# A decoder layer whose residual is turned from rows of tokens to rows of channels

## The chip, the core and the metric

The kernel runs on one core of a Trainium2 chip. A core has a matmul engine (TensorE, PE in the profile; PEld is its loading of weights), a vector engine (VectorE, DVE), an activation engine (ScalarE, ACT), GpSimd (POOL) and a sync engine (SP). SP and POOL do hardly any arithmetic here: they issue DMA transfers, each in its own written order, and 16 DMA engines carry these. Matmuls multiply a stationary operand (the weights, at most 128x128) with a moving one (up to 512 columns) into one of eight PSUM banks of 128 x 512 fp32. All data are fp32, and one matmul in the program is two records in the trace.

The metric is the device time of one call in microseconds (us). Lower is better.

## What is computed

One layer of a decoder for a prompt of 256 tokens and 8 samples of one token each, so 264 tokens, of width 2048. Cut to what matters:

```python
def _rms(x, g):                       # three times: before mix, cross, experts
    return x * rsqrt(mean(x * x, -1) + EPS) * g
z = _rms(x, g_mix) @ w_in             # 2048 -> q 768 | k 768 | v 768 | u 1280
# q, k, v: 12 heads of 64, QK-norm, window attention with bias; a sample reads
#   its cache of 2048 keys at three dilations (128, 97 and 96 rows matter)
# u: 4 groups x 320; trailing mean over 2/4/8/16 tokens minus the token,
#   then a 320x320 map per group and a scale per channel
x = x + concat(attention, pooled) @ w_out          # 2048 -> 2048
q = rms_heads(_rms(x, g_cross) @ w_cq)             # 4 heads of 128
x = x + cross_attention(q, mem_k, mem_v) @ w_co    # 256 memory rows
x = x + experts(_rms(x, g_ffn))       # top 1 of 4 groups, top 2 of 8 experts
```

The caches of window keys and values are outputs too: 8 samples x 2 caches of 6141 KB, copied from DRAM to DRAM. Each of the 32 experts has 12.6 MB of weights, and all are read.

## The kernel before

There is no scheduler: each engine has its own hand-written list of instructions, and semaphores tie the lists together. The work runs in stages:

1. Constants, the memory rows and `x` are loaded. `norm_turn` (L634) normalises and turns rows at once: a matmul with a 128x128 block of rows stationary and a diagonal matrix of scales moving. DVE puts the result into `hT` in `norm_rows` (L1325), times the gain.
2. `project` (L640) multiplies with w_ck and w_cv (memory keys and values), then with w_in in seven chunks of 512 columns. The 128 tokens of a tile are stationary, 512 weight columns stream past, 16 k-steps for each of two token tiles; the eight samples come by themselves in `project_sample` (L647). Six matmuls (L705) turn the bias between chunks. During chunks 4 to 6 `query_row` (L679) spreads a sample's query over 128 partitions, and DVE multiplies and sums it with the keys (`sample_scores`, L1352 and L1355).
3. `attend` runs the 12 heads one after another: `score_win`, `turn_win`, `value_win`.
4. Pooling is done on PE: `pool_channels` (L789 to L792) multiplies `u` with constant matrices; `pool_map` (L810) applies the maps. `values_of` (L819) sums each sample's values.
5. w_out in four chunks, again by `project` and `project_sample`; DVE adds the rows to the residual `x3`.
6. `norm_turn`, w_cq, cross attention of four heads; w_co, with the samples' cross attention between (L679, L819).
7. `norm_turn`, the router (L941), and then 32 experts in a loop: gather (L969), gate and up (L1028), down (L1053), combine (L993).

The residual `x3` lies by tokens: 128 tokens on the partitions, 2048 channels along each.

SP brings the large weights through a ring of two slots of 4 MB (`big`, L391): the piece i + 2 is issued when piece i has been used by PE. Once w_cq and w_co have been used, their two slots take the first expert's gate and up halves (L470), and the stream of expert weights begins: each half is fetched again when the expert before has used it. POOL issues the sixteen cache copies (`cache_copy`, L531), each after a named weight piece has landed, and between them, in one list, the rows of window keys and values (`window_rows`, L541 to L544) and of the memory caches (L594). A POOL instruction that waits holds everything behind it in this list.

Of the kernel before, what the change touches and what calls it, by code (L numbers as in the profile page):

```python
# [8 lines left out]
F32 = mybir.dt.float32  # L9
# [6 lines left out]
P = 128  # L16
# [6 lines left out]
TC = SEQ + 32  # L23
# [32 lines left out]
def bias_columns(dist):  # L56
# [3 lines left out]
    for c, d in enumerate(dist):  # L60
# [4 lines left out]
        else:  # L65
# [10 lines left out]
CONST_W = dict(ident=P, tri=P, moe=NE + NE + 3 + OVB + BLK, pool=PG * 256 + PG * P, pools=2 * PG * NB,  # L76
               flip=P, mask=AW, xmask=XW, sel=4, ohp=384, ohs=NDEC)
# [8 lines left out]
def constants():  # L86
# [17 lines left out]
    full = np.zeros((PG, SEQ, SEQ), np.float32)  # L104
    for g, w in enumerate(POOL_WINDOWS):
        for t in range(SEQ):
            lo = max(t + 1 - w, 0)
            full[g, lo:t + 1, t] = 1.0 / min(w, t + 1)
            full[g, t, t] -= 1.0
    pool = part("pool")  # L110
    pool[:, 0:PG * 256] = full[:, 0:P].transpose(1, 0, 2).reshape(P, -1)
    pool[:, PG * 256:] = full[:, P:, P:].transpose(1, 0, 2).reshape(P, -1)
    ps = part("pools").reshape(P, 2, PG, NB)
    for g, w in enumerate(POOL_WINDOWS):
        for b in range(NB):
            ps[b * HIST + HIST - (w - 1):b * HIST + HIST, 0, g, b] = 1.0 / w
            ps[b, 1, g, b] = 1.0 / w - 1.0
    for i in range(4):
        for h in range(H):
            part("mask")[32 * i + h, h * HD:(h + 1) * HD] = 1.0  # L120
        for h in range(XH):
            part("xmask")[32 * i + h, h * XD:(h + 1) * XD] = 1.0
        part("sel")[32 * i:32 * i + 32, i] = 1.0
    part("ohp")[0:NBUCKET + 1] = bias_columns([255 - v for v in range(384)])
    part("ohs")[0:NBUCKET + 1] = bias_columns(DEC_DIST)
    return c


def hybrid_decoder_layer(nc, a):
    with ExitStack() as ctx:  # L130
# [3 lines left out]
        def sb(name, shape, dt=F32):  # L134
            return ctx.enter_context(nc.sbuf_tensor(name, shape, dt))

        bias_dram = nc.dram_tensor("bias_rows", (H, 384), F32, kind="Internal").ap()


        ring = sb("ring", [P, 3, 8192])
        x3 = sb("x3", [P, 3, D])
        hT = sb("hT", [P, KT, TC])
        z = sb("z", [P, 3, IN_W])
        qkm = sb("qkm", [P, 4096])
        mkT = qkm[:, H * SEQ:].rearrange("p (h m) -> p h m", h=XH)
        qkT = qkm[:, 0:H * SEQ].rearrange("p (a h t) -> p a h t", a=2, h=H // 2)
        ident = sb("ident", [P, P])
        tri = sb("tri", [P, P])  # L150
        dg = sb("dg", [P, 3, P])
# [3 lines left out]
        poolsc = sb("poolsc", [P, 2, PG, NB])  # L155
        sel = sb("sel", [P, 4])
        gT = sb("gT", [P, 4, KT])
        gqk = sb("gqk", [P, 2, HD])
        gxx = sb("gxx", [P, 2, XD])
        psc = sb("psc", [P, PW // P])  # L160
        st = sb("st", [P, 152])
# [3 lines left out]


        slot2 = ring[:, 2, :]
        mixT = slot2[:, 0:KT * TC].rearrange("p (k t) -> p k t", k=KT)
        hmT = slot2[:, 0:KT * NM].rearrange("p (k t) -> p k t", k=KT)
        AFTER_MIX = KT * TC  # L170
        bias = slot2[:, AFTER_MIX:AFTER_MIX + H * SEQ].rearrange("p (h j) -> p h j", h=H)
        bias_flat = after_mix = slot2[:, AFTER_MIX:AFTER_MIX + H * SEQ]
        biasS = slot2[:, AFTER_MIX + H * SEQ:AFTER_MIX + H * SEQ + NDEC]
        qkt_flat = qkm[:, 0:H * SEQ]
        rb = psm[:, 0, 0:H]
        rbs = psm[:, 0, 16:144].rearrange("p (i h) -> p i h", i=4)
        flip = slot2[:, 8192 - P:8192]
        hankel = qkt_flat
        ohp = qkt_flat[:, 0:384]
        ohs = qkt_flat[:, 384:384 + NDEC]  # L180
        brow = qkt_flat[:, 768:768 + 384]
        sq = qkt_flat[:, 1536:1536 + 2 * AW]
        zf = z[:].rearrange("p t n -> p (t n)")
# [6 lines left out]
        pw = pslot[:, 0:10 * PC].rearrange("p (c d) -> p c d", c=10)  # L190
        poolT = pslot[:, 3200:3200 + 10 * TOK].rearrange("p (c t) -> p c t", c=10)
        state = pslot[:, 5840:5840 + PW]
        poolc = z[:, 0, 0:2 * AW]
        poolA = poolc[:, 0:1024].rearrange("p (g t) -> p g t", g=PG)
        poolB = poolc[:, 1024:1536].rearrange("p (g t) -> p g t", g=PG)
        prb = z[:, 1, 0:768].rearrange("p (b j) -> p b j", b=2)
        prT = z[:, 1, 768:1536].rearrange("p (b j) -> p b j", b=2)
        h_flat = hT[:].rearrange("p k t -> p (k t)")

        kbuf, vbuf = ([r[:, lo:lo + 3 * AW].rearrange("p (t n) -> p t n", t=3) for r, lo in rs]  # L200
                      for rs in (((slot2, 0), (slot2, 3 * AW)), ((h_flat, 0), (h_flat, 3 * AW), (qkt_flat, 0))))
        norm_dump = h_flat[:, 0:D]
        mask = after_mix[:, 0:AW]
        masked = after_mix[:, AW:2 * AW]

        memr = zf[:, 0:2 * D].rearrange("p (t n) -> p t n", t=2)
        msq = zf[:, 2 * D:2 * D + XW]
        mk = z[:, 2, IN_W - 4 * XW:IN_W - 2 * XW].rearrange("p (t n) -> p t n", t=2)
        mv = z[:, 2, IN_W - 2 * XW:IN_W].rearrange("p (t n) -> p t n", t=2)
        xq = zf[:, 0:3 * XW].rearrange("p (t n) -> p t n", t=3)  # L210
        xqT = zf[:, 1536:1536 + XH * SEQ].rearrange("p (h t) -> p h t", h=XH)
        xsq = zf[:, 2560:2560 + XW]
        oT = slot2[:, 0:XH * TC].rearrange("p (h t) -> p h t", h=XH)
        xprb = slot2[:, 1152:2176].rearrange("p (b j) -> p b j", b=2)
        xprT = slot2[:, 2176:3200].rearrange("p (b j) -> p b j", b=2)

# [74 lines left out]
        def wk(i):  # L291

            return ring[:, i % 2, :].rearrange("p (k n) -> p k n", k=KT)
# [1452 lines left out]
```

## Time and profile before

| | us |
|---|---|
| median of 3 runs | 1753.99 |
| range of the runs | 1750.31 to 1757.3 |
| the profiled execution, its own time | 1755.72 |
| its span in the trace | 1753.9 |
| PE busy in it | 1395.7 |
| PE loading weights | 659.6 |
| DVE busy | 582.6 |
| ACT busy | 177.0 |
| POOL busy | 55.2 |

The span leaves out 1.8 us that lie around it. Busy times of PE and PEld overlap. A busy share over the whole span mixes stages with different limits, so the stages are to be read one by one. In a view by windows, the granted clock is a share of TensorE's full speed, and the DMA share is the mean busy share of the 16 DMA engines.

### The profile page before, as it was taken

How to read it: one execution, taken by the hardware profiler on the slowest of the kernel's cores; microseconds unless marked ns; L12 is line 12 of the kernel's file. 1: busy time of each engine (PE TensorE's matmuls, PEld its weight loads, DVE VectorE, ACT ScalarE, POOL GpSimd, SP SyncE). 2: the span in 40 equal slices, each digit the busy share in tenths (PEclk: the TensorE clock that was granted, in tenths of full speed). 3: DMA queues.
4: the chain of work that ended last, by engine and by line, in shares of the span. 5: the costliest groups of instructions: out<-in, count | busy, mean ns of one | idle time of the engine just before them, and what ended most of it. 6: DMA issues, size and time to landing. Idle time of an engine off the chain costs nothing.

```text
span 1753.9 us, 24539 instructions
## 1 busy us (share of the span) xinstructions
PE 1395.7 (80%) x10597; PEld 659.6 (38%) x10597; DVE 582.6 (33%) x1157; ACT 177.0 (10%) x439; POOL 55.2 (3%) x103
## 2 busy tenths in 40 slices
PE   5999999889999987885867777777677776767675
PEld 4474454445454564462322222222232222222222
DVE  2120244352000023644433434343434343434344
ACT  2000010033100003110000000000000000000000
POOL 0000011111110000100000000000000000000000
PEclk9999999977999998986988989898989898999898
DMA  7997479989289999553999999999999999999996
GB/s 304 332 327 247 155 247 358 274 303 293 78 281 330 336 335 342 185 215 137 413 427 424 428 424 428 425 428 424 428 424 428 424 428 425 427 425 427 426 427 265
DMA packets 80539, 607.56 MB, mean 346 GB/s; under 512 B 12128, under 2 KB 15662, under 8 KB 44493
## 3 DMA queue, kind: packets, MB, share of 16 engines
q1 hardware_dynamic: 72349, 480.87, 67.2%
q0 software_dynamic: 8144, 126.02, 21.2%
q8 instruction: 36, 0.59, 0.1%
q14 instruction: 10, 0.08, 0.0%
HBM read 601.84 MB, written 106.16 MB: 404 GB/s over the span
## 4 chain that ended last, share of the span: by engine, by line
PE 48%; DMA 45%; DVE 4%; SPq 1%; issue 1%; ACT 1%; DVEq 0%; POOL 0%; ACTq 0%
DMA ring<-in_w_e_up_dram 41%; PE pb L640 22%; PE pb L1028 9%; PE pb L634 4%; DMA ring<-in_w_in_dram 3%; PE pb L647 2%; PE pb L819 2%; PE pb L810 1%; SPq L470 1%; PE pb L679 1%; PE pb L775 1%; PE pb L766 1%; PE pb L969 0%; PE pb L941 0%; PE pb L789 0%
## 5 line engine op out<-in xcount | busy, mean ns | idle before, releaser
L1028 PE MATMUL pb<-ring,z 128*32 128x256 f32 x4096 | 310.8, 471 | 194.5 <-DMA ring<-in_w_e_up_dram 193.8
L1679 DVE TENSOR_TENSOR x<-pb,x 128x512 f32<-128x512 f32 (+1 forms) x384 | 237.5, 678 | 398.6 <-PE pb L993 398.6
L1028 PEld LDWEIGHTS pb<-ring,z 128*32 128x32 f32 x4096 | 153.6, 134 | 375.2 <-DMA ring<-in_w_e_up_dram 245.8
L640 PE MATMUL pb<-ring,hT 128*128 128x512 f32 x512 | 227.0, 603 | 10.7 <-DMA ring<-in_w_in_dram 9.6
L640 PE MATMUL pb<-ring 128*128 128x512 f32 x448 | 196.7, 598 | 1.6 <-DVE ring L1325 0.8
L640 PEld LDWEIGHTS pb<-ring,hT 128*128 128x128 f32 x512 | 98.3, 194 | 132.3 <-issue 121.2
L640 PEld LDWEIGHTS pb<-ring 128*128 128x128 f32 x448 | 85.3, 192 | 108.1 <-issue 106.2
L1053 PE MATMUL pb<-ring,z 128*32 128x512 f32 x992 | 114.6, 603 | 0.0
L993 PE MATMUL pb<-z 32*128 32x512 f32 (+1 forms) x768 | 106.0, 622 | 3.9 <-issue 2.2
L969 PE MATMUL pb<-z 128*32 128x512 f32 (+1 forms) x792 | 100.1, 620 | 6.3 <-DVE z L1658 6.3
L634 PE MATMUL pb<-dg,x 128*128 128x128 f32 x288 | 64.3, 392 | 17.2 <-DVE dg L1316 17.2
L634 PEld LDWEIGHTS pb<-dg,x 128*128 128x128 f32 x288 | 63.4, 312 | 20.1 <-DVE dg L1316 18.0
L1262 ACT ACTIVATE z<-pb 128x128 f32<-128x128 f32 x32 | 8.9, 277 | 521.3 <-PE pb L1028 521.3
L1691 DVE TENSOR_SCALAR z<-z 128x128 f32<-128x128 f32 x32 | 7.3, 227 | 160.4 <-ACT z L1262 160.4
L1486 DVE TENSOR_TENSOR x<-pb,x 128x512 f32<-128x512 f32 x16 | 11.1, 692 | 123.1 <-PE pb L640 123.1
L1053 PEld LDWEIGHTS pb<-ring,z 128*32 128x32 f32 x992 | 29.5, 111 | 57.6 <-issue 57.0
L1417 DVE COPY z<-pb 128x512 f32<-128x512 f32 x7 | 4.8, 691 | 124.7 <-PE pb L640 124.7
L1034 PE MATMUL pb<-ident,z 128*128 128x128 f32 x32 | 10.7, 334 | 40.4 <-DVE z L1697 40.4
L969 PEld LDWEIGHTS pb<-z 128*32 128x32 f32 (+1 forms) x792 | 19.3, 109 | 60.4 <-issue 50.3
L977 PE MATMUL pb<-ident,z 128*128 128x128 f32 x132 | 21.2, 285 | 26.1 <-ACT z L1258 26.1
L993 PEld LDWEIGHTS pb<-z 32*128 32x128 f32 (+1 forms) x768 | 23.8, 149 | 36.7 <-issue 34.1
L1352 DVE TENSOR_TENSOR ring<-ring,pb 128x1536 f32<-128x1536 f32 (+1 forms) x16 | 20.9, 1350 | 48.4 <-PE pb L679 48.4
(251 smaller groups left out, 1017.2 us busy)
## 6 DMA issues: line engine op xcount, KB each, us to landing
ring<-in_w_e_gate_dram SPq DMA_DIRECT2D x64, 2048.0 KB, 19.0
ring<-in_w_e_up_dram SPq DMA_DIRECT2D x64, 2048.0 KB, 23.5
ring<-in_w_e_down_dram SPq DMA_DIRECT2D x31, 4096.0 KB, 22.1
out_win_k_sample_dram<-in_cache_win_k_dram POOLq DMA_DIRECT2D x8, 6141.0 KB, 22.3
out_win_v_sample_dram<-in_cache_win_v_dram POOLq DMA_DIRECT2D x8, 6141.0 KB, 24.7
ring<-in_w_in_dram SPq DMA_DIRECT2D x7, 4096.0 KB, 16.7
ring<-in_w_out_dram SPq DMA_DIRECT2D x4, 4096.0 KB, 17.5
ring<-in_cache_win_k_dram POOLq DMA_DIRECT2D x16, 288.0 KB, 8.3
```

Of the source, the lines that this page charges most:

```text
L470: sp.dma_start(ring[:, half, 4096 * m:4096 * m + 4096].rearrange("p (k n) -> p k n", k=8), src.rearrange("(p k) n -> p k n", k=KT)[:, 8 * ...
L634: last = mm(bk[:, P * k:P * k + P], cols[:, 4 * j + k, :], dg[:, t, :], start=True, stop=True)
L640: last = mm(bk[:, :], xT[:, k, tile * P:tile * P + P], w[:, k, :], start=(k == 0), stop=(k == nk - 1))
L647: last = mm(bk[32 * c:32 * c + 32, 0:P], xT[:, k, SEQ:TC], w[:, k, P * c:P * c + P], start=(k == 0), stop=(k == nk - 1))
L819: last = mm(bk[32 * i:32 * i + 32, 0:n], s_in[0:k, t, hf, 32 * i:32 * i + 32], buf[0:k, t, lo:lo + n], start=(t == 0), stop=(t == len(tile ...
L969: last = mm(pb[0][32 * c:32 * c + 32, :], pick[0:n, t, :], xn[0:n, t, 512 * c:512 * c + 512], start=(t == 0), stop=(t == 2))
L977: last = nc.tensor.transpose(pb[0][:, P * j:P * j + P], xe[:, P * j:P * j + P], ident[:])
L993: last = mm(banks[c][0:n, :], GT[r, P * t:P * t + n], yo[r, :], start=True, stop=True)
L1028: last = mm(pb[1][32 * c:32 * c + 32, 0:256], XT[:, k % 4, 32 * (k // 4):32 * (k // 4) + 32], w[:, :, k8, P * c:P * c + P], start=(k == 0) ...
L1053: last = mm(pb[3][32 * c:32 * c + 32, :], aT[:, 32 * f:32 * f + 32], w[f][:, 512 * c:512 * c + 512], start=(f == 0), stop=(f == 3))
L1352: V.tensor_tensor(src, src, filled()[:, 0:n].unsqueeze(1).to_broadcast([P, tiles, n]), ALU.mult)\
L1679: last = V.tensor_tensor(d, banks[c][0:n, :], d, ALU.add)
```

## The change

The residual is kept by channels instead, as `xT`: 128 channels on the partitions, 16 blocks of channels, 264 tokens along each.

- Rows are turned once, by plain transposes of `x` and of the memory rows; the norms' scales are spread by a matmul with ones, and DVE writes `hT` in 16 instructions of 264 columns (`scaled_rows`). Sums of squares come from ACT squares, added up on DVE.
- The projections onto `u`, w_out, w_cq and w_co keep a 128x128 block of weights stationary and stream the 264 tokens past it, prompt and samples together: `channels` (10 tiles of 16 steps), the w_out loop (16 tiles of 16), `cross_query` (4 of 16), the w_co loop (16 of 4). The projections onto q, k, v (four and a half chunks of w_in) and of the memory stay as they were.
- Window attention goes by pairs of heads, and its steps stand between the tiles of `channels`.
- Pooling's trailing sums are shifted adds on DVE (`pool_sums`, `pool_mean`), and only the samples' old state goes over PE.
- The samples' queries are stored in DRAM and read back by a DMA that spreads them over 128 partitions (`qrep`); `query_row` is gone, and so are the matrices of constants and masks that were loaded for pooling and for `own_heads`.
- The samples' window values go in three column groups of one bank. Their cross attention is grouped: the keys are transposed between the w_out tiles, and one bank takes all samples' scores.
- The router's matmuls take the residual by channels and run beside the w_co tiles; for the experts the rows are turned back to tokens.
- POOL's list is written anew. The expert loop and the order of its weights are as they were; two of the cache copies now wait until the first expert's first half has landed.

PE's list in window attention. Before, one head after another (L759 and L760 scores, L766 turns of the probabilities, L775 and L776 values):

```order
L759 MATMUL pb<-qkm 128x128
L760 MATMUL pb<-qkm 128x256
L766 MATMUL pb<-ident,z 128x128 x3
L775 MATMUL pb<-z 64x256
L776 MATMUL pb<-z 64x128
```

In the changed kernel, at the same place, with L737 the channel tile, L784 the values, L775 the turns and L766 the scores of a pair:

```order
L784 MATMUL pb<-Z 64x256 x2
L784 MATMUL pb<-Z 64x128 x2
L775 MATMUL pb<-ident,Z 128x128 x6
L766 MATMUL pb<-qkm 128x128 x2
L766 MATMUL pb<-qkm 128x256 x2
L737 MATMUL pb<-hreg,ring 128x264 x16
```

The five steps of one head, which followed those of the head before, have become the steps of three different pairs with a whole weight tile behind them.

POOL's list at the fifth and sixth cache copies, with the semaphore that an entry waits for (w_landed is a landed weight piece, keys_used a sample's keys used by DVE). Before:

```order
L531 DMA out_win_k_sample_dram<-in_cache_win_k_dram 96x16376 [waits w_landed1]
L541 DMA ring<-in_cache_win_k_dram 128x768 [waits keys_used]
L542 DMA ring<-in_cache_win_k_dram 96x768
L543 DMA ring<-in_cache_win_k_dram 96x768
L544 DMA ring<-z 1x16x48
L541 DMA ring<-in_cache_win_k_dram 128x768 [waits keys_used]
```

And in the changed kernel, where L550 is the copy and L564 the spread query:

```order
L550 DMA out_win_v_sample_dram<-in_cache_win_v_dram 96x16376 [waits w_landed0]
L554 DMA ring<-in_cache_win_k_dram 128x768 [waits keys_used]
L555 DMA ring<-in_cache_win_k_dram 96x768
L556 DMA ring<-in_cache_win_k_dram 96x768
L557 DMA ring<-out_win_k_sample_dram 1x16x48
L564 DMA Z<-sample_queries 128x768
L554 DMA ring<-in_cache_win_k_dram 128x768 [waits keys_used]
```

The rows of keys still stand behind a copy in one list, with one more transfer for each sample, and the next copy stands behind two samples' rows instead of three.

PE's list at the end of w_out. Before, L640 the prompt, L647 the samples, L634 the norm:

```order
L640 MATMUL pb<-ring 128x512 x32
L647 MATMUL pb<-ring 32x128 x64
L634 MATMUL pb<-dg,x 128x128 x48
L640 MATMUL pb<-ring,hT 128x512 x16
```

In the changed kernel, with L890 the w_out tile, L897 the turn of memory keys, L901 the norm's sum and L909 the cross query:

```order
L890 MATMUL pb<-hreg,ring 128x264 x10
L890 MATMUL pb<-Z,ring 128x264 x6
L897 MATMUL pb<-ident,qkm 128x128 x4
L901 MATMUL pb<-Z,ones 128x264
L909 MATMUL pb<-hreg,ring 128x264 x32
```

The 48 norm matmuls between w_out and w_cq have become one, and the turns of the memory keys have come into the w_out loop.

The diff, cut to its core:

```diff
-            def norm_turn(rows, first, end, parts=range(4), new_scales=True):
-                for t in range(first, end):
-                    cols = rows[:, t, :].rearrange("p (m k) -> p k m", k=KT)
-                    for j in parts:
-                        bk = vbank()
-                        for k in range(4):
-                            last = mm(bk[:, P * k:P * k + P], cols[:, 4 * j + k, :], dg[:, t, :], start=True, stop=True)
+            for k in range(KT):
+                bk = abank("x")
+                for t in range(2):
+                    turn(bk[:, P * t:P * t + P], xraw[:, t, P * k:P * k + P], ident[:])
+                turn(bk[:, SEQ:TOK], xraw[0:NB, 2, P * k:P * k + P], ident[0:NB, 0:NB]).then_inc(a_filled, 1)
...
-            def norm_rows(first, end, gain, dst, parts=range(4)):
-                        V.tensor_tensor(dst[:, 4 * j:4 * j + 4, P * t:P * t + n], src,
-                                        gT[:, gain, 4 * j:4 * j + 4].unsqueeze(2).to_broadcast([P, 4, n]), ALU.mult)\
+            def scaled_rows(i):
+                for k in range(KT):
+                    V.scalar_tensor_tensor(out=hT[:, k, :], in0=xT[:, k, :], scalar=gT[:, KT * i + k:KT * i + k + 1], in1=rbc[:],
+                                           op0=ALU.mult, op1=ALU.mult).then_inc(h_ready, 1)
...
-            for n in range(NCH):
-                project_sample(hT, wk(i), KT, abank(), a_filled)
+            for n in range(5):
+                width = 512 if n < 4 else 256
+                project_sample(wk(IN0 + n), abank("sin"), width // 4)
...
+            def channels(j):
+                c = 2 + j
+                if c % 4 == 0:
+                    piece_landed(pe, IN0 + 4 + c // 4)
+                w = wk(IN0 + 4 + c // 4)[:, :, P * (c % 4):P * (c % 4) + P]
+                bk = abank("u")
+                for k in range(KT):
+                    last = mm(bk[:, 0:TOK], w[:, k, :], hT[:, k, :], start=(k == 0), stop=(k == KT - 1))
+                last.then_inc(a_filled, 1)
...
-            attend(H, score_win, turn_win, value_win)
+            channels(3)
+            channel_rows(0, 3)
+            value(0)
+            turn_probs(1)
+            score(2)
...
-            def query_row(rows, lo, n, b):
-                mm(bk[:, 0:n], ident[:, b:b + 1].to_broadcast([P, P]), rows[:, 2, lo:lo + n], start=True, stop=True)\
+                pool.dma_start(qrep[:, b % 2], qs_dram[b:b + 1, :].to_broadcast([P, AW])).then_inc(key_landed[b % 2], 16)
...
+                link(TT(rows, rows, qrep[:, b % 2].unsqueeze(1).to_broadcast([P, 3, AW]), ALU.mult))
...
-            def pool_channels(c):
-                    mm(bk[o, 0:SEQ], z[:, 0, u], poolA[:, g, :], start=True, stop=False)
-                    mm(bk[o, P:SEQ], z[:, 1, u], poolB[:, g, :], start=False, stop=True)
-                    mm(bk[o, SEQ:TOK], state[0:NB * HIST, us], poolsc[0:NB * HIST, 0, g, :], start=True, stop=False)
-                    last = mm(bk[o, SEQ:TOK], z[0:NB, 2, u], poolsc[0:NB, 1, g, :], start=False, stop=True)
+            def pool_sums(tiles, levels, only_last=None):
+                link(TT(S0[:, 0:n, 1:UC], uT[:, j0:j0 + n, 1:UC], uT[:, j0:j0 + n, 0:UC - 1], ALU.add))
+                for lv in range(1, levels):
+                    src, dst = (S0, S1) if lv % 2 else (S1, S0)
+                    link(TT(dst[:, i, lo:UC], src[:, i, lo:UC], src[:, i, lo - d:UC - d], ALU.add))
...
-                        last = mm(bk[32 * i:32 * i + 32, 0:n], s_in[0:k, t, hf, 32 * i:32 * i + 32],
-                                  buf[0:k, t, lo:lo + n], start=(t == 0), stop=(t == len(tiles) - 1))
+                    for g in range(VG):
+                        last = mm(sv[32 * g:32 * g + 32, 0:VC], pvals(t, n, b, g), vbuf[b % 3][0:n, t, VC * g:VC * g + VC],
+                                  start=(b == 0 and t == 0), stop=(b == NB - 1 and t == 2))
...
-                project(mixT, wk(i), KT, 0, vbank(), v_filled)
-                project(mixT, wk(i), KT, 1, vbank(), v_filled)
-                project_sample(mixT, wk(i), KT, vbank(), v_filled)
+            for o in range(KT):
+                w = wk(WOUT + o // 4)[:, :, P * (o % 4):P * (o % 4) + P]
+                    last = mm(bk[:, 0:TOK], w[:, k, :], mix(k), start=(i == 0), stop=(i == KT - 1))
+                if t == 0:
+                    pe.wait_ge(xk_landed[b % 2], 16 * (b // 2 + 1))
+                    last = turn(bk[:, P * h:P * h + P], xk[b % 2][:, t, XD * h:XD * h + XD], ident[:])
...
-                    query_row(xq, 0, XW, 2 * n + t)
+                    last = mm(bk[32 * h:32 * h + NB, 0:NM], qown[:, h, b, :], KT8[:, b, h, :], start=(b == 0), stop=(b == NB - 1))
...
-                    project(oT, wo[:, :, 512 * n:512 * n + 512], XH, t, vbank(), v_filled)
+                    last = mm(pb[o % 4][:, 0:TOK], wo[:, h, P * o:P * o + P], oT[:, h, :], start=(h == 0), stop=(h == XH - 1))
+                last = mm(pb[4][0:36, 0:TOK], wr[:, k, :], xT[:, k, :], start=(k == 0), stop=(k == KT - 1))
...
-                    for i in range(10, 16):
-                        piece_landed(pool, WOUT + (2, 3, 4, 4, 5, 5)[i - 10])
-                        cache_copy(i)
+            for i in range(14, 16):
+                pool.wait_ge(gu_landed[0], 32)
+                cache_copy(i)
```

## Rows read from the trace of the kernel before

**Rows 1.** The page's own line of busy times, and the chain's shares by line.
```profile
PE 1395.7 (80%) x10597; PEld 659.6 (38%) x10597; DVE 582.6 (33%) x1157; ACT 177.0 (10%) x439; POOL 55.2 (3%) x103
...
DMA ring<-in_w_e_up_dram 41%; PE pb L640 22%; PE pb L1028 9%; PE pb L634 4%; DMA ring<-in_w_in_dram 3%; PE pb L647 2%; PE pb L819 2%; PE pb L810 1%; SPq L470 1%; PE pb L679 1%; PE pb L775 1%; PE pb L766 1%; PE pb L969 0%; PE pb L941 0%; PE pb L789 0%
```

**Rows 2.** Timeline of SP's queue: start, us, engine, line, transfer.
```profile
823.98 0.34 SPq L470 DMA_DIRECT2D ring<-in_w_e_gate_dram  x1
```

**Rows 3.** Windows: stretch, length, busy PE, PEld, DVE, ACT, POOL; clock, DMA share, GB/s.
```profile
0.00:824.00 824.00, 736.05 (x3757) 407.63 (x3761) 224.89 (x458) 110.12 (x279) 55.18 (x103) 0.93 0.77 266
...
113.40:363.30 249.90, 240.33 (x1398) 119.47 (x1399) 69.22 (x58) 16.30 (x41) 19.75 (x38) 0.98 0.77 256
363.30:419.00 55.70, 48.19 (x175) 29.48 (x172) 27.68 (x107) 28.46 (x90) 7.36 (x15) 0.60 1.00 339
419.00:487.40 68.40, 67.62 (x276) 34.10 (x275) 2.04 (x4) 8.56 (x21) 11.04 (x21) 1.00 0.42 126
487.40:614.30 126.90, 126.89 (x768) 62.64 (x768) 8.95 (x20) 6.50 (x18) 6.76 (x11) 0.99 0.93 327
614.30:697.50 83.20, 67.05 (x345) 46.97 (x345) 26.32 (x67) 18.43 (x46) 1.01 (x2) 0.90 0.97 342
697.50:783.40 85.90, 69.91 (x360) 44.34 (x360) 45.84 (x76) 13.96 (x38) 7.85 (x11) 0.90 0.51 190
783.40:824.00 40.60, 22.07 (x141) 9.70 (x145) 19.12 (x79) 1.00 (x3) 0.00 (x0) 0.66 0.32 127
824.00:1754.00 930.00, 659.64 (x6848) 252.01 (x6840) 357.75 (x699) 66.93 (x160) 0.00 (x0) 0.90 0.99 417
```

**Rows 4.** Chain of waits, first 125 us: start, us, what.
```profile
20.67 14.25 PE pb L634 x64
...
35.69 55.20 PE pb L640 x128
90.89 20.86 PE pb L634 x96
111.74 0.87 PE pb L672 x8
```

**Rows 5.** The same chain over the whole span.
```profile
113.39 13.97 PE pb L640 x32
...
277.87 47.84 DMA ring<-in_w_in_dram
```

**Rows 6.** Timeline of PE, three short stretches.
```profile
447.84 0.94 PE L810 MATMUL pb<-ring 128*128 128x264 f32 x3 [0.47 <-ACT ring L1183]
...
447.84 1.16 PE L810 MATMUL pb<-ring 128*128 128x264 f32 x4 [0.47 <-ACT ring L1183]
...
783.43 7.31 PE L941 MATMUL pb<-hT,z 128*36 128x264 f32 x32 [0.38 <-DVE hT L1325]
...
419.32 4.07 PE L819 MATMUL pb<-hT,s_in 128*32 128x512 f32 x12
```

**Rows 7.** Groups of VectorE by form: busy us, mean ns.
```profile
L1352 DVE TENSOR_TENSOR ring<-ring,pb 128x768 f32<-128x768 f32 x8 | 7.6, 947 | 0.0
...
L1465 DVE SCALAR_TENSOR_TENSOR z<-pb,ring 128x256 f32<-128x256 f32 x12 | 5.0, 413 | 0.0
```

**Rows 8.** DMA issues with us to landing: page, line L391, and window 373 to 440.
```profile
out_win_k_sample_dram<-in_cache_win_k_dram POOLq DMA_DIRECT2D x8, 6141.0 KB, 22.3
...
DMA to landing us min/median/max: 13.5/19.0/62.4
...
ring<-in_w_out_dram SPq DMA_DIRECT2D x1, 4096.0 KB, 62.4
```

**Rows 9.** Chain of waits, 600 to 860 us.
```profile
620.29 21.24 PE pb L634 x96
...
697.48 3.70 PE pb L640 x8
701.18 0.86 PE pb L679 x2
```

More of the change, by code:

```diff
@@ L198, in hybrid_decoder_layer @@
[L198 to L208, printed above, removed]
@@ L465, in gate_up @@
+            for i in range(WOUT + 1, CO + 1):
+                big(i)
             def gate_up(i, e, half):
@@ new lines, in score @@
+            def score(p):
+                if p == 0:
+                    pe.wait_ge(a_freed, a_at("qk", 5))
+                banks = [vbank("score"), vbank("score")]
+                for lo, rows, n in ((0, slice(0, P), P), (P, slice(P, SEQ), SEQ)):
+                    for i in range(2):
+                        r = slice(64 * i, 64 * i + 64)
+                        last = mm(banks[i][:, lo:lo + n], qkT[r, 0, p, rows], qkT[r, 1, p, 0:n], start=True, stop=True)
+                        if lo:
+                            last.then_inc(v_filled, 1)
@@ L795, in pool_map @@
+            piece_landed(pe, POOLW)
+            pe.wait_ge(state_landed, 16)
+            bk = vbank("state")
+            for g in range(PG):
+                for j, r, n in GROUP[g]:
+                    last = mm(bk[r:r + n, NB * j:NB * j + NB], state[0:NB * HIST, P * j + r:P * j + r + n],
+                              poolsc[0:NB * HIST, g, :], start=True, stop=True)
+            last.then_inc(v_filled, 1)
             def pool_map(kt):
-                bk = abank()
+                pe.wait_ge(pooled, 1 if kt < 7 else 2)
+                bk = abank("map")
+                parts = []
@@ new lines, in _ @@
+            last.then_inc(a_filled, 1)
+            cross_turn(2)
+            cross_value(1)
+            pe.wait_ge(a_freed, a_at("xsturn"))
+            pe.wait_ge(xv_landed, 16 * NB)
+            bk = abank("xsvals")
+            for b in range(NB):
+                for t in range(2):
+                    for h in range(XH):
+                        last = mm(bk[32 * h:32 * h + NB, 0:XD], pown[:, t, h, b, :], xv[b][:, t, XD * h:XD * h + XD],
+                                  start=(b == 0 and t == 0), stop=(b == NB - 1 and t == 1))
@@ new lines, in _, with channels, channel_rows @@
+                for c in range(4):
+                    last = copy(z[0:NB, 2, 512 * n + w * c:512 * n + w * c + w], bk[32 * c:32 * c + NB, 0:w])
+                freed(last)
+            def channels(j):
+                freed(copy(uT[:, j, PAD:UW], filled("u")[:, 0:TOK]))
+            def channel_rows(first, end):
+                bk = filled("uout")
+                for j in range(first, end):
+                    r, lo = (32, 2 * AW + P * j) if j < 6 else (64, 2 * AW + P * (j - 6))
+                    last = copy(z[r:r + 32, 2, lo:lo + P], bk[0:32, P * (j - first):P * (j - first) + P])
+                freed(last)
@@ new lines, in _ @@
+            cross_exps(2)
+            cross_turned(1)
+            cross_exps(3)
+            act.wait_ge(s_biased, 3)
+            nc.scalar.activation(xps, VB[(v_at("xsscore") - 1) % 4][:, 0:NM], ACT.Exp, bias=st[:, 112:113], scale=-1.0,
+                                 accum_out=st[:, 114:115]).then_inc(s_exped, 1)
+            cross_value(0)
+            bk = filled("xsturn")[:, 0:2 * P].rearrange("p (t h c) -> p t h c", t=2, h=XH)
+            act.wait_ge(own_zero, 1)
+            for t in range(2):
+                last = copy(p_flat[:, t, :, 0:NB * NB:NB + 1], bk[:, t, :, 0:NB])
```

1695 lines of the change are left out of this document (925 added, 770 removed).

## The prediction

> **What bounds the kernel now.** I read the page first [rows 1]: PE is busy for 80% of the span, but the chain's largest entry is a DMA, the experts' up weights, with 41%. A mean over two different programs, then, and the question is where they meet. SP's queue gives the place: at 823.98 us it issues the first weights of the expert stream [rows 2]. The windows show what each half is limited by [rows 3]. From 824 to the end, 930 us, the DMA engines are busy for 0.99 of the time at 417 GB/s: that half lasts as long as its weights take. Before it, PE is busy for 736 of 824 us, and the DMA engines for only 0.77. So
>
> time = start of the expert stream + 930,
>
> and all that the change can win lies before the start. The change leaves the experts, their weights and their order alone, so 930 stays. What can pull the start forward is PE's path, and what can stop it is the DMA work ahead of the start: 0.77 x 824 = 634 us of fully busy engines [rows 3]. Hence two sums: PE's path without any wait for DMA, and then the waits.
>
> **PE's path, part by part.** The price of the new form, 264 columns with a new 128x128 weight for every record: three such records take 0.94 us and four 1.16 [rows 6], so one more costs 0.22; the router's 32 records (36 weight columns) take 7.31, 0.228 each [rows 6]. I take 0.222; a tile of 16 steps (32 records) is 7.1 us.
>
> 1. Entry. The 20.86 us of norm matmuls for `x` between the memory projections and w_in go [rows 4]. In their place 48 transposes stand ahead of the memory projections, at 0.109 each (8 in 0.87 [rows 4]) 5.2 us, with 32 for the memory rows, 3.5 us; together less than the 14.25 that 64 records take there now [rows 4], though the loads and the statistics come first as before. I let the memory projections start at 37 instead of 35.7, add 55.2 and 3 us for a slower clock and eight key transposes: w_in starts at 95 instead of 113.4. The 16 scaled writes on DVE (413 ns for 256 columns [rows 7], so 6.8 us) lie beside the memory projections.
> 2. q, k, v: the first chunk's tile takes 13.97 [rows 5]; with the other tile and the samples a chunk is 31.2. Four chunks 125, half a chunk 17, the bias matmuls 5: 147, to 242.
> 3. Channels and attention. Ten tiles are 71 us. Before, attention's stretch of 55.7 us had PE busy for 48.2 at a granted clock of 0.60 [rows 3], so at full clock at most 29; two heads of a pair now use different halves of the array, for which I take 22. With 3 for turns, 96: to 338. The pooling matrices go; 12 shifted adds and some ten small corrections on DVE cost about 16 us (947 ns for 768 columns [rows 7]) on an engine busy for 27.7 of 55.7 there, and hide behind the tiles, save the last group, which the maps wait for; 2 us for that.
> 4. Samples' values, state and maps took 68.4 [rows 3]. The constants' matmuls leave; a sample's values, 12 records of up to 512 columns in 4.07 [rows 6], become 18 of 256 in three column groups, about 1.5 to 2; ten maps about 1.8. Sum 34: to 372.
> 5. w_out: 16 tiles 114, and 64 key transposes 7: 121 instead of 126.9 [rows 3], to 493. The gain is small: 264 columns in place of two times 512 and the samples' pass, but a new weight each time. DVE adds each tile to the residual and ACT squares it, some 0.4 to 0.5 us of 264 columns each [rows 7], beside 7.1 of PE.
> 6. Norm, w_cq and cross attention: 83.2 before [rows 3]. The 21.24 of norm matmuls [rows 9] go; one sum, a root and 16 paced writes (12 us, the first query tile rides along), three more tiles (21), heads and grouped samples (33): 66, to 559.
> 7. w_co: 128 records 28.4, router 7.3, turning back 5.2: 41, to 600, instead of 85.9 [rows 3]. The query rows (0.86 after each 3.70 of w_co [rows 9]) and the samples' pass are gone.
> 8. Router to first half used: 40.6 before [rows 3], less the 7.3 that moved up and 2 of norm, is 31; plus 6 for building the rows and scales again: 637.
>
> PE's path alone would start the stream at 637, 187 us earlier, and end at 1567.
>
> **What of that the DMA engines give back.** Their work ahead of the start grows by the spread queries (8 x 0.39 MB) and shrinks by constants and masks: I take 634 + 5 = 639, with 634 and 650 as bounds. A path of 637 with 639 of transfers under it would need engines that never rest, and the order forbids that: the ring has two slots, a weight piece is issued only when one is free, and copies are issued when a weight piece lands. A cache copy takes 22.3 us to land [rows 8], and while one runs a weight piece hardly advances: a piece needs 13.5 alone, but 47.84 behind a copy and key rows [rows 5], 62.4 behind others at the worst [rows 8]. Today that costs PE one long wait; the pieces will now be used every 28 to 31 us as before, but the stages between, which gave the engines time (419 to 487 at a DMA share of 0.42, 697 to 783 at 0.51 [rows 3]), shrink by half. Walking the queues by these prices:
> - the third channel tile waits for w_in's sixth piece, behind the sixth copy and key rows: 12 us;
> - the turns of pairs 1 and 4 stand behind DVE's sample scores in DVE's list, and these behind key rows that POOL issues after a copy: 17 and 15 us. What is held there is PE's list, and all later tiles;
> - in w_out the memory keys stand in POOL's list behind copies, and PE's key transposes wait for them between the tiles: 14 us;
> - 13 us for a lower granted clock after such waits (0.60 to 0.90 in the stretches that have them now, 0.99 to 1.00 in those that don't [rows 3]).
>
> Sum 71: the start moves to 708. As a check, the DMA engines then rest for 708 - 639 = 69 us ahead of the start, against 190 now (a share of 0.90 instead of 0.77). Bounds: no waits, 637; all the rest kept, share 0.77, 639 / 0.77 = 830.
>
> 708 + 930 = 1638 of span; the 1.8 us around it and the profiled run's distance from the median (1755.72 against 1753.99) cancel. Forecast **1638 us**, 6.6% faster; its own range is 1600 to 1680, for waits of 33 to 113 us.
>
> **A rule against the change.** Both forms take a fresh weight in every record. A record of 512 columns takes 13.97/32 = 0.437 us [rows 5], one of 264 takes 0.222 [rows 6]; 0.437 x 264/512 is 0.225, so the time goes with the columns and nothing is left over for the load. The Trainium skill, page "TensorE: Matmul & The Clock Gate", Part 3 "The mechanism", says that a weight load overlaps a running matmul only when the two use different row groups; these use the same 128 rows. By its section "LDWEIGHTS (loading the stationary operand)" a load of 128 columns takes 107 ns, an estimate from which would make a record 0.33. The trace does not bear this out; I keep it as a rival, since a run of four is short and the router's weights have only 36 columns.
>
> **Rivals.**
> - *PE's path alone decides* (1565 to 1600). For it: in 487 to 614 PE is busy for 126.89 of 126.90 us with the DMA at 0.93 [rows 3]. Against: it would want the DMA engines at 0.95 and more over the whole first part, which no long stretch there has.
> - *More waits* (1680 to 1745): a share of about 0.86, start 743, 1673, and upward to 0.78, 1749. For it: the waits couple, since a late PE frees a slot late, the piece after it lands late, and so does the copy that waits for it. Against: copies have been spread so that their rows come sooner in POOL's list.
> - *Nothing won* (1745 to 1763): the DMA share stays at 0.77, start 830.
> - *Loads not hidden*: 1088 records (320 channels, 512 w_out, 128 w_cq, 128 w_co) at 0.105 more are 114 us on PE's path, of which half falls into the waits: start about 768, 1698. The router's 32 records at 0.228 speak against it [rows 6].
> - *Slower, by the clock*: in 363 to 419 a PE with small matmuls between waits had a granted clock of 0.60 [rows 3]. If the many short waits kept it there through channels, w_out, cross and w_co, some 340 us of matmuls at full clock would take 340/0.60 = 567: path 637 + 227 = 864, end 1794. It decides from 297 + 340/c = 824, a clock of 0.65. For it: attention's steps now stand between the tiles. Against: the same stages as dense tiles hold 0.98 to 1.00 [rows 3], and the tiles are now in among the small steps.
>
> **How the numbers follow.** Forecast 0.60; PE's path alone 0.13; more waits 0.14; loads not hidden 0.04; nothing won 0.03; slower by the clock 0.06. A difference of 0.5%, 8.8 us, is about what a measurement of this kernel can tell from none. Faster by more: 0.60 + 0.13 + 0.14 + 0.04 = 0.91; within it 0.03; slower 0.06. The range 1580 to 1715 leaves out under half of PE's path alone (0.05), under half of more waits (0.06) and the last two (0.09): 2 in 10.
>
> **What would show it.** In the changed trace the first SP issue of the second expert's gate weights should stand near 708, with 930 after it. The channel and w_out tiles should take 7.1 us each (10.6 if loads are not hidden). The window from the start of w_in should begin near 95. PE's idle time should be put down to window key rows, the sixth piece of w_in and memory keys, some 55 to 60 us in all, and the DMA share ahead of the start should be near 0.90. I am wrong if the tiles are slow, if the start lies above 790 or below 650, or if the part after it is not 930.

## The result and the profile after

The changed kernel takes 1649.79 us (median of 4 runs, 1648.75 to 1652.41), against 1752.6 us for the kernel before, timed beside it: a ratio of 0.9412, 95% interval 0.9389 to 0.9436, or 5.9% faster. The forecast was 1638, with a range of 1580 to 1715. The profiled run has a span of 1648.1 us.

First the place where the two programs meet. SP's timeline of the changed kernel (start, us, engine, line, transfer), the row that answers to [rows 2]:

```profile
715.46 0.33 SPq L489 DMA_DIRECT2D ring<-in_w_e_gate_dram  x1
```

The stream starts 108.5 us earlier than before, and 932.6 us follow it, where 930 did. The time is won ahead of the stream, all of it. The windows of the changed kernel, cut where its stages begin (columns as in [rows 3]):

```profile
0.00:98.10 98.10, 78.38 (x228) 40.33 (x229) 23.18 (x57) 22.02 (x37) 1.36 (x6) 0.91 0.90 304
98.10:243.20 145.10, 145.10 (x969) 77.09 (x968) 37.04 (x34) 13.37 (x33) 12.63 (x24) 1.00 0.94 329
243.20:380.90 137.70, 101.79 (x507) 81.22 (x505) 60.04 (x122) 30.44 (x101) 18.49 (x35) 0.85 0.96 311
380.90:423.30 42.40, 38.83 (x245) 19.56 (x243) 5.88 (x16) 5.31 (x13) 13.94 (x25) 0.88 0.87 268
423.30:564.50 141.20, 126.65 (x576) 106.92 (x576) 12.61 (x32) 14.20 (x32) 10.07 (x15) 0.94 0.84 298
564.50:630.70 66.20, 54.73 (x381) 41.66 (x381) 24.36 (x46) 15.65 (x43) 2.19 (x5) 0.87 0.94 354
630.70:674.60 43.90, 43.85 (x196) 29.17 (x196) 12.12 (x31) 11.04 (x25) 0.00 (x0) 1.00 1.00 363
674.60:715.50 40.90, 15.08 (x128) 7.72 (x131) 17.36 (x80) 16.57 (x13) 0.00 (x0) 0.62 0.42 180
715.50:1648.00 932.50, 658.92 (x6848) 252.36 (x6840) 357.82 (x699) 67.16 (x160) 0.00 (x0) 0.90 0.99 416
```

Read the PE column against the length. In q, k and v (98 to 243), and in w_co (631 to 675), PE is busy throughout. In channels and attention (243 to 381) it is busy for 101.8 of 137.7 us at a clock of 0.85, with the DMA engines at 0.96: there PE waits for DMA. In the last 41 us ahead of the stream PE is busy for 15.1, and the DMA engines have a share of 0.42.

What PE waits for, the four longest between w_in and the stream (engine, line, tile, what it waits for: us in all, times, longest):

```profile
PE pb L775 <- DVEq L1569: 25.4, 2, 16.4
PE pb L1034 <- DVE xT L1794: 15.2, 1, 15.2
PE pb L897 <- DMA qkm<-in_cache_mem_k_dram: 14.0, 3, 7.9
PE pb L737 <- DMA ring<-in_w_in_dram: 9.8, 1, 9.8
```

The first row names DVE, but the chain of waits shows what DVE had waited for (start, us, what; the sixth piece of w_in, the two waits for spread queries, one wait for memory keys in w_out with the weight piece ahead of it, and a w_out tile):

```profile
228.41 43.31 DMA ring<-in_w_in_dram
...
274.58 27.00 DMA Z<-sample_queries
...
320.11 23.17 DMA Z<-sample_queries
...
477.84 7.14 PE pb L890 x32
484.99 28.99 DMA ring<-in_w_out_dram
514.81 23.55 DMA qkm<-in_cache_mem_k_dram
```

The spread query of a sample is the last transfer of its key rows. It took 27.0 and 23.2 us behind cache copies that POOL had issued 2.6 and 5.4 us earlier; in the run without copies below it lands after 4.4 to 11.7 us. In w_out the order is the same: POOL waits for the weight piece, issues a copy at 514.27, and the memory keys come behind it. The row of L890 is a w_out tile: 32 records in 7.14 us, 0.223 each.

A wait costs PE more than its own length. The tile behind the wait for w_in's piece ran at a mean granted clock of 0.74, the next one at 1.00; from PE's timeline, in which a tile at the full clock takes 7.3 to 7.4:

```profile
271.77 9.88 PE L737 MATMUL pb<-hreg,ring 128*128 128x264 f32 x32 [9.75 <-DMA ring<-in_w_in_dram]
...
283.09 7.39 PE L737 MATMUL pb<-hreg,ring 128*128 128x264 f32 x32
```

### The profile page after: what moved, and what is told of

It is laid out like the page before. It is cut to its first block, busy times and chain, and to the rows that moved or that the text cites. A ratio compares the mean times of both kernels' runs of the same rounds, so it can differ in the third digit from the quotient of the medians.

```text
span 1648.1 us, 23510 instructions
## 1 busy us (share of the span) xinstructions
PE 1263.3 (77%) x10061; PEld 656.0 (40%) x10061; DVE 550.4 (33%) x1117; ACT 195.8 (12%) x454; POOL 58.7 (4%) x109
## 4 chain that ended last, share of the span: by engine, by line
DMA 54%; PE 37%; DVE 4%; SPq 2%; ACT 2%; issue 1%; POOL 0%; DVEq 0%; POOLq 0%; ACTq 0%
DMA ring<-in_w_e_up_dram 43%; PE pb L1111 11%; PE pb L663 10%; PE pb L890 4%; DMA Z<-sample_queries 3%; DMA qkm<-in_cache_mem_k_dram 3%; DMA ring<-in_w_in_dram 3%; PE pb L909 2%; PE pb L1009 2%; DMA ring<-in_w_out_dram 2%; SPq L429 1%; PE pb L858 1%; PE pb L737 1%; PE pb L669 1%; SPq L489 1%
## 5 line engine op out<-in xcount | busy, mean ns | idle before, releaser
L1111 PE MATMUL pb<-ring,xT 128*32 128x256 f32 x4096 | 312.8, 473 | 197.7 <-DMA ring<-in_w_e_up_dram 196.9
L1868 DVE TENSOR_TENSOR Z<-pb,Z 128x512 f32<-128x512 f32 (+1 forms) x384 | 237.6, 679 | 389.9 <-PE pb L1076 389.9
L1111 PEld LDWEIGHTS pb<-ring,xT 128*32 128x32 f32 x4096 | 154.9, 135 | 378.9 <-DMA ring<-in_w_e_up_dram 248.1
L663 PE MATMUL pb<-ring,hreg 128*128 128x512 f32 (+1 forms) x320 | 125.3, 551 | 0.0
L1136 PE MATMUL pb<-ring,xT 128*32 128x512 f32 x992 | 112.8, 595 | 0.0
L1076 PE MATMUL pb<-xT 32*128 32x512 f32 (+1 forms) x768 | 106.0, 622 | 3.8 <-issue 2.1
L1052 PE MATMUL pb<-Z,xT 128*32 128x512 f32 (+1 forms) x792 | 97.9, 608 | 6.3 <-DVE xT L1847 6.3
L737 PE MATMUL pb<-hreg,ring 128*128 128x264 f32 x320 | 78.9, 408 | 9.8 <-DMA ring<-in_w_in_dram 9.8
L890 PE MATMUL pb<-hreg,ring 128*128 128x264 f32 x320 | 77.9, 401 | 0.3 <-ACT Z L1302 0.3
L737 PEld LDWEIGHTS pb<-hreg,ring 128*128 128x128 f32 x320 | 63.9, 202 | 23.9 <-DMA ring<-in_w_in_dram 10.2
L890 PEld LDWEIGHTS pb<-hreg,ring 128*128 128x128 f32 x320 | 62.5, 200 | 10.9 <-issue 0.4
L663 PE MATMUL pb<-ring 128*128 128x512 f32 x128 | 57.8, 615 | 0.0
L1136 PEld LDWEIGHTS pb<-ring,xT 128*32 128x32 f32 x992 | 29.1, 109 | 56.3 <-issue 55.6
L890 PE MATMUL pb<-Z,ring 128*128 128x264 f32 x192 | 45.3, 386 | 0.0
L890 PEld LDWEIGHTS pb<-Z,ring 128*128 128x128 f32 x192 | 36.5, 190 | 6.2
```

The lines of the kernel that those rows point to most:

```text
L663: last = mm(bk[:, 0:n], xt[:, k, tile * P:tile * P + P], w[:, k, 0:n], start=(k == 0), stop=(k == KT - 1))
L737: last = mm(bk[:, 0:TOK], w[:, k, :], hT[:, k, :], start=(k == 0), stop=(k == KT - 1))
L890: last = mm(bk[:, 0:TOK], w[:, k, :], mix(k), start=(i == 0), stop=(i == KT - 1))
L1052: last = mm(pb[0][32 * c:32 * c + 32, :], pick[0:n, t, :], xn[0:n, t, 512 * c:512 * c + 512], start=(t == 0), stop=(t == 2))
L1076: last = mm(banks[c][0:n, :], GT[r, P * t:P * t + n], yo[r, :], start=True, stop=True)
L1111: last = mm(pb[1][32 * c:32 * c + 32, 0:256], XT[:, k % 4, 32 * (k // 4):32 * (k // 4) + 32], w[:, :, k8, P * c:P * c + P], start=(k == 0) ...
```

## Experiments

Each run is timed beside the kernel before. Where several runs were taken, the median and the ratio to the kernel before are given; the two can differ by some us when they are set against the changed kernel, and then both are named.

**1. The changed kernel without copies.**

```diff
-                pool.dma_start(dst.rearrange("(p f) -> p f", p=96), src.rearrange("(p f) -> p f", p=96)).then_inc(copied, 16)
+                return
```

> The changed kernel without its sixteen cache copies (98 MB that it then does not move; the two sample cache outputs stay unwritten). Theory: the start of the expert stream is PE's path plus what DMA takes from it. In the changed kernel PE idles 25.4 us for sample scores held by key rows, 9.8 for the sixth piece of w_in, 14.0 for memory keys and about 3 for value rows, and runs some 10 us slower after these. Without copies all of that goes: start from 715 to about 652, time about 1586 (1575 to 1605). Rival: the waits come from the order of the lists on PE, DVE and ACT, not from the copies: start stays above 700, time above 1630.

1587.2 us (one run); the stream starts at 651.63, as expected. The theory holds and the rival falls. The windows, cut at the same stages:

```profile
0.00:96.70 96.70, 76.26 (x228) 38.76 (x229) 22.81 (x57) 21.89 (x37) 0.20 (x4) 0.93 0.59 200
96.70:242.90 146.20, 146.20 (x975) 78.07 (x974) 37.24 (x35) 13.47 (x33) 10.72 (x20) 1.00 0.53 183
242.90:336.70 93.80, 92.48 (x500) 74.52 (x499) 60.12 (x122) 30.23 (x101) 17.01 (x32) 1.00 0.61 189
336.70:378.90 42.20, 37.42 (x246) 19.12 (x245) 5.87 (x16) 5.30 (x13) 13.89 (x25) 0.92 0.83 269
378.90:501.10 122.20, 121.18 (x576) 103.53 (x576) 13.03 (x33) 14.37 (x33) 8.48 (x12) 1.00 0.53 191
501.10:566.90 65.80, 54.83 (x382) 41.84 (x382) 23.92 (x45) 15.11 (x41) 0.00 (x0) 0.87 0.49 198
566.90:610.80 43.90, 43.90 (x197) 29.15 (x197) 12.12 (x31) 11.04 (x25) 0.00 (x0) 1.00 0.14 52
610.80:651.60 40.80, 14.97 (x123) 7.63 (x127) 17.34 (x80) 16.57 (x13) 0.00 (x0) 0.62 0.36 150
```

Behind the entry PE waits for DMA for only 4.5 us here, all of it at the values, so this is the direct measure of the first of the two sums of the prediction. The run takes away both the copies' share of the engines and their place in POOL's list; it doesn't part the two. The copies cost the changed kernel 63.9 us of its path: 43.9 in channels and attention, 19.0 in w_out, 1 in the rest.

**2. The kernel before without copies.** The same edit to the kernel before.

> The kernel before, without its sixteen cache copies (same part left out). Theory: its PE path is the limit there, DMA only takes the wait for w_in's sixth piece and w_out's start (about 10 us of idle PE, and a low clock after it): 1725 to 1742, so far less than the same cut gives in the changed kernel. Rival: the kernel before was held by DMA as much as the changed one is: about 1690.

1743.39 us (one run), 10 us less than with copies and 1.4 outside the expected stretch; the stream starts at 809.01, 15 us earlier. The rival (1690) falls. The same 98 MB that hold the changed kernel back by 63 us cost the kernel before 10: it was PE's, and the changed one is PE's and DMA's together.

**3. Every channel tile twice.**

```diff
-                for k in range(KT):
+                for k in [*range(KT), *range(KT)]:
```

> The changed kernel with every channel tile computed twice into the same bank (the second pass starts afresh, so the values are the same): 71 us more of matmul between the steps of attention. Theory: 35 us of PE's waits there (pairs 1 and 4, sixth piece) are for DMA and are filled by the extra work, and the clock stays up: 25 to 45 us slower, about 1685. Rival: PE's list is the limit there and the waits move along: 65 to 71 slower, about 1718.

1680.15 us (one run), 30 us more for 71 us of added matmul, inside the expected 25 to 45. The rest went into waits that vanished: PE is busy for 163.5 of 164.7 us of this stage at full clock.

```profile
243.80:408.50 164.70, 163.53 (x819) 135.41 (x818) 60.12 (x122) 30.33 (x101) 18.42 (x35) 1.00 0.81 260
```

So the changed kernel's channel stage had some 41 us of free PE time, lost to waits and to the lower clock that came with them; the run without copies gives 43.9 for the same stage.

**4. The experts' rows behind the router.**

```diff
             rows_back(3)
+            act.wait_ge(exp_in, 1)
+            nc.scalar.activation(rt[:, 1300:1312], rt[:, 1300:1312], ACT.Exp).then_inc(exp_out, 1)
+            act.wait_ge(exp_in, 2)
+            nc.scalar.activation(rt[:, 1312:1315], rt[:, 1312:1315], ACT.Exp).then_inc(exp_out, 1)
+
             act.wait_ge(scale_ready, 1)
             act.wait_ge(back_copied, 12)
...
                               st[0:n, 9 + t:10 + t]).then_inc(xn_ready, 1)
-
-            act.wait_ge(exp_in, 1)
-            nc.scalar.activation(rt[:, 1300:1312], rt[:, 1300:1312], ACT.Exp).then_inc(exp_out, 1)
-            act.wait_ge(exp_in, 2)
-            nc.scalar.activation(rt[:, 1312:1315], rt[:, 1312:1315], ACT.Exp).then_inc(exp_out, 1)
```

> The changed kernel with ACT's three writes of the experts' rows (11.0 us) put behind the router's two exponentials instead of ahead of them. In the changed kernel DVE waits 7.7 us for the first exponential. Theory: the stream's start comes forward by that: 6 to 8 us faster, about 1642.5. Rival: the second half of the first expert's weights, which lands at 689, or the rows, then 3 us later than needed, hold it: 0 to 2 us.

1640.71 us (1633.55 to 1643.8), ratio 0.934 (0.9317 to 0.9363): 9 us faster than the changed kernel by the medians, 13 by the ratios, for an expected 6 to 8; in the profiled runs the stream starts 6.1 us earlier, at 709.38. The rival (0 to 2) falls. What had stood there, from the changed kernel's timeline (start, us, engine, line, out, in, count):

```profile
678.08 11.00 ACT L1393 ACTIVATE Z<-Z,st 128x2048 f32<-128x2048 f32 x3
...
689.10 1.28 ACT L1397 ACT_TABLE_LOAD   x1
690.39 0.21 ACT L1397 ACTIVATE xT<-xT 128x12 f32<-128x12 f32 x1
690.71 0.17 DVE L1784 TENSOR_REDUCE xT<-xT 128x3 f32<-128x12 f32 x1 [7.72 <-ACT xT L1397]
```

DVE waited 7.72 us for an exponential of 0.21 us that stood in ACT's list behind 11 us of rows and 1.28 of loading a table of functions. With the order turned round, PE's wait for the router (15.2 us) is 7.5.

**5. Attention behind the channel tiles.** PE's list is shown; those of ACT and DVE are reordered to match it.

```diff
-            channels(1)
-            score(0)
-            channels(2)
-            turn_probs(0)
+            for j in range(1, 4):
+                channels(j)
+            channel_rows(0, 3)
...
+            score(0)
+            score(1)
+            turn_probs(0)
+            for p in range(2, PAIRS):
+                score(p)
+                value(p - 2)
+                turn_probs(p - 1)
```

> The changed kernel with window attention behind all ten channel tiles instead of between them, as it was before the change (DVE scores samples 3 to 7 beside the tiles, then does the heads). Theory: the tiles between the steps covered the heads' DVE and ACT work, but they also put DVE's sample scores, and so the key rows behind copies, into PE's way. Undone, the tiles run through but for the sixth piece (71 + 13), the last sample's keys still come only near 343, and 35 to 45 us of heads follow: 5 to 15 us slower than the changed kernel, 1655 to 1665. Rival: the interleaving is worth what attention by itself costs, 25 us or more (1675 and up). Second rival: it costs more than it covers, and undoing it is faster.

1667.25 us (1660.06 to 1667.7), ratio 0.9488 (0.9458 to 0.9518): slower than the changed kernel by 17 us in the medians, 2 over the expected stretch, and by 13 in the ratios, inside it; either way below the first rival's. So interleaving pays, by less than attention costs by itself. In the profiled run the stream starts 17.3 us later, at 732.72. The stage takes 147.0 us in place of 137.7, with PE busy for 103.4 of them, and the values behind it 50.7 in place of 42.4, at a clock of 0.76 instead of 0.88:

```profile
242.30:389.30 147.00, 103.37 (x499) 81.88 (x498) 53.55 (x112) 29.31 (x97) 18.41 (x35) 0.85 0.85 278
389.30:440.00 50.70, 43.36 (x248) 22.00 (x247) 12.78 (x27) 5.59 (x17) 13.93 (x25) 0.76 0.86 265
```

PE waits 21.2 us for w_in's pieces and 18.8 behind DVE here, 9.8 and 25.4 in the changed kernel. That the sample scores in PE's way are what keeps interleaving from paying more is not shown by this run.

**6. Copies cut in two between the rows.**

```diff
+            key_rows(4)
             piece_landed(pool, IN0 + 5)
-            cache_copy(6)
...
+            cache_copy(6, (0,))
+            key_rows(5)
+            cache_copy(6, (1,))
...
+                    h = b - 1
+                    cache_copy(9 + h // 2, (h % 2,))
```

> The changed kernel with the rows after the router (as in the fourth run), and with copies 6 to 11 cut into two halves each that stand between single samples' rows in POOL's list: the same bytes, but no row stands behind more than half a copy (about 10 us). Theory: PE's waits for key rows (25.4 us) and for memory keys (14.0) fall to less than half: 15 to 30 us faster than the fourth run, 1612 to 1626. Rival: the engines carry the same bytes and a weight piece or a row comes late elsewhere instead, the DMA share ahead of the start stays at 0.89: within 5 us of the fourth run, 1636 to 1646.

1647.05 us (1642.19 to 1647.82), ratio 0.9377 (0.9354 to 0.9401): no faster than the fourth run, rather slower (6 us), and 1 us above the rival's stretch. The theory failed, in the way its rival said. PE's waits in this run (columns as above):

```profile
PE pb L897 <- DMA ring<-in_w_out_dram: 21.3, 1, 21.3
PE pb L782 <- DVEq L1576: 17.3, 2, 12.9
PE pb L744 <- DMA ring<-in_w_in_dram: 13.1, 1, 13.1
PE pb L875 <- DMA ring<-Z: 9.6, 2, 8.1
```

The waits for memory keys are gone and those for key rows are smaller, but a w_out piece now comes 21.3 us late, w_in's piece 13.1 and the value rows 9.6. The DMA share ahead of the start is 0.88. The order of these transfers decided who waits; the sum did not fall: 61.3 us for these four rows, against 52.5 for key rows, memory keys, w_in's piece and value rows in the fourth run.

**7. The kernel before with plain turns.**

```diff
-                        last = mm(bk[:, P * k:P * k + P], cols[:, 4 * j + k, :], dg[:, t, :], start=True, stop=True)
+                        last = nc.tensor.transpose(bk[:, P * k:P * k + P], cols[:, 4 * j + k, :], ident[:])
```

> The kernel before with each norm matmul against the diagonal of scales replaced by a plain transpose (leaves out the norms' scale factors). One record in place of two: memory rows, x, cross and router turn in about half the time or as fast as DVE empties a bank (0.69 us): some 8.5 + 12.5 + 13 + 9 us of PE's path go. Theory: PE's path was the limit there, the DMA share of 0.77 leaves room, and it comes through whole: 1708 to 1716. Rival: the DMA engines give half of it back, as in the changed kernel: 1728 to 1735.

1714.42 us (one run), inside the stretch of the theory. The stream starts at 778.32, 45.7 us earlier, for some 43 expected to leave PE's path, and the time is 39.5 us shorter, mostly since the part behind the start took 934 us in this run instead of 930. The DMA share ahead of the start rises from 0.77 to 0.81: the kernel before had room for it.

**8. Copies one place later.** On top of the fourth run:

```diff
-            for b in range(4, 7):
+            for b in range(4, NB):
                 key_rows(b)
-            piece_landed(pool, IN0 + 6)
-            cache_copy(7)
-            key_rows(7)
...
-            cache_copy(8)
+            cache_copy(7)
...
+            piece_landed(pool, CQ)
+            cache_copy(11)
             pool.wait_ge(v_filled, v_at("out", KT - 1))
             memory_rows(1, 7, xv[7], xv_landed)
...
+            pool.wait_ge(gu_landed[1], 32)
+            cache_copy(15)
```

> The kernel of the fourth run with the copies from the seventh on moved one place back in POOL's list: none stands between the samples' key rows 4 to 7 but one, the twelfth is issued when w_cq has landed (ahead of the last memory rows, not behind them), and the last waits for the second half of the first expert. Same bytes. The fourth run's DMA engines rest for 16 us in its last 34 us before the stream and for 23 us in w_out; without copies the start was 652. Theory: rest that is filled there is taken off PE's waits: the wait of pair 4 (about 15 us) goes, and little comes back: start from 709 to 695 to 700, time 1626 to 1634. Rival (as the half copies showed): another wait takes its place, 1636 to 1646.

1628.1 us (1623.79 to 1630.88), ratio 0.9286 (0.927 to 0.9302). As expected; it beats both kernels. The stream starts at 694.12. The first part of this run, its last 33 us ahead of the stream, and the same stage in the fourth run:

```profile
0.00:695.00 695.00, 603.51 (x3237) 401.82 (x3241) 192.57 (x418) 128.33 (x294) 58.57 (x109) 0.92 0.91 317
661.20:694.10 32.90, 14.77 (x126) 7.35 (x128) 17.36 (x80) 16.48 (x13) 0.51 (x1) 0.69 0.96 375
...
675.00:709.00 34.00, 15.88 (x119) 7.50 (x123) 17.36 (x80) 16.48 (x13) 0.00 (x0) 0.60 0.51 216
```

The share of that stage goes from 0.51 to 0.96. PE's waits for key rows fall from 25.7 to 16.8 us, and the four waits counted for the fourth run from 52.5 to 39.6 together. The difference to the sixth run: there the same bytes stayed in the same stages, here they moved into time in which little else was carried.

**9. The seventh copy behind all key rows too.**

```diff
-            piece_landed(pool, IN0 + 5)
-            cache_copy(6)
             for b in range(4, NB):
                 key_rows(b)
+            piece_landed(pool, IN0 + 6)
+            cache_copy(6)
```

> As the eighth run, and the seventh copy too stands behind the last key rows and the last piece of w_in instead of behind the sixth piece. Theory: both waits for key rows (25 us) and part of the wait for the last w_in piece go, the value rows come later by half a copy: 8 to 14 us faster than the eighth run, 1614 to 1624. Rival: with a copy less ahead of it the engines rest in attention, and what is put off is paid in w_out or at the values: within 4 us of the eighth run.

On top of the eighth run. 1630.0 us (1620.04 to 1640.62), ratio 0.93 (0.9269 to 0.933): no different from the eighth run, as the rival had it. PE's waits of this run:

```profile
PE pb L896 <- DMA qkm<-in_cache_mem_k_dram: 14.9, 3, 6.7
PE pb L736 <- DMA ring<-in_w_in_dram: 14.9, 1, 14.9
PE pb L867 <- DMA ring<-Z: 14.2, 3, 10.7
```

The wait for key rows (16.8 us in the eighth run) is gone and stands elsewhere: 14.2 us for value rows, and 14.9 instead of 5.9 for w_in's piece.

## Why the prediction was right

Its frame held: time is the start of the expert stream plus a nearly constant rest, 932.6 us for 930 (929.9 to 934.2 over all traces of this case). The two sums that make the start can be held against the windows of the run without copies and of the changed kernel:

| stage, us | predicted path | without copies | changed kernel |
|---|---|---|---|
| to w_in | 95 | 96.7 | 98.1 |
| q, k, v | 147 | 146.2 | 145.1 |
| channels, attention | 96 | 93.8 | 137.7 |
| values, state, maps | 34 | 42.2 | 42.4 |
| w_out | 121 | 122.2 | 141.2 |
| norm, w_cq, cross | 66 | 65.8 | 66.2 |
| w_co, router's sums | 41 | 43.9 | 43.9 |
| router to the stream | 37 | 40.8 | 40.9 |
| start | 637 | 651.6 | 715.5 |

- *PE's path* was 14.6 us too short. More than half is one term, the values: 42.2 instead of 34. The price of a sample was right where the clock is full (18 records in 1.50 us, 1.5 to 2 forecast), but the first two samples took 2.78 each at the lower clock, and value rows come late even without copies (PE is busy for 37.4 of the 42.2 us). The prediction let nothing wait there and had the clock full.
- *Router to the stream*: 3.8 too short. The 6 us for building rows and scales were taken as one sum beside the rest; that the 11 us of rows stood ahead of the router's exponentials in ACT's list was not seen. The fourth run shows what it was worth: 7.7 us of PE's wait, 9 to 13 of the time.
- *What the DMA engines give back*: 71 forecast, 63.9 measured. Their places were right: pairs 1 and 4 behind sample keys and the sixth piece of w_in (12 + 17 + 15 forecast, 25.4 + 9.8 measured), memory keys in w_out (14 forecast, 14.0 measured), 49.2 of waits in all for 58. The clock was put at 13; in channels and in w_out PE's own busy time is 9.3 and 5.5 us longer than without copies, at 0.85 and 0.94 instead of 1.00. Value rows cost nothing on top: 3.3 us of waits with copies, 4.5 without. The DMA share ahead of the start was 0.89 for a forecast 0.90.
- *The sum*: a path 14.6 too short, a give-back 7.1 too large and 2.6 more behind the start leave 10.1 of span. That the first two errors partly cancel is luck.
- *PE's path alone decides* fell: the share it needed, 0.98 (639 of 651.6), was not reached by any order tried; the best had 0.91 and 0.92 (the last two runs). One reason given against it was weak, though: [rows 3] has a stretch of 83 us at 0.97, and the changed kernel has 138 us at 0.96.
- *More waits* and *nothing won* fell by size: the share rose from 0.77 to 0.89.
- *Loads not hidden* fell: a tile takes 7.12 to 7.16 us, 0.223 for a record, in row after row: a load between two of them cost nothing that shows. The trace so disagrees, for these fp32 records on the same 128 rows, with the sentence of the Trainium skill, page "TensorE: Matmul & The Clock Gate", Part 3 "The mechanism", by which a load overlaps a running matmul only when the row groups differ. The same section also lets a load go ahead that targets the background weight buffer; the prediction left that out, and no run here shows whether it is the reason.
- *Slower by the clock* fell: the clock ahead of the start was 0.91, and 0.85 in the channel stage. There the tiles right behind a wait were slow (9.88 us above), those that followed were not (7.39); the run with tiles twice, in which PE hardly waits in this stage, has 1.00.

## What to carry to other kernels

When a bound is shared by two engines, sum each one's path and then walk the waits; the gain is what is left after both. Work taken from the longer path comes through whole only while the other has room: some 40 us did in the kernel before, while the changed kernel lost 63 us to copies that had cost the old one 10. Background transfers are better moved into stretches that carry little, not cut up within a stretch that is full; and a small result that others wait for should not stand behind long writes in one engine's list.

## What was not expected of the hardware

Removing copies of 98 MB took 291 us of DMA share off the first part of the changed kernel (0.89 x 715.4 less 0.53 x 651.6), 18 us for each, while its time fell by 63. A spread read of a 3 KB row to 128 partitions took 23 to 27 us behind a copy; the runs don't show whether a queue of its own would have spared it, since every transfer of POOL went through one. The lower clock behind a wait did not cost in proportion to it: PE's three long waits in the channel stage, 9.75, 16.39 and 9.04 us, were followed by matmuls that took 2.6, 3.0 and 2.7 us more than the same ones elsewhere in the stage.
